# First layer of a two-block kernel: the state-space output is moved and used block by block from SyncE, and the first convolution taps go to ScalarE

## The reference, cut to what matters

```python
proj = x @ w_in                                   # 1024 -> 1536
xm, zm, us = proj[..., :512], proj[..., 512:1024], proj[..., 1024:]
xc = silu(causal_dwconv(xm, conv_w, conv_b))      # 4 taps
q, k, v = block-diagonal products of xc, xc, xm
gates = concat([q, k, v]) @ w_if + b_if
h = mlstm_chunkwise(q, k, v, i_pre, f_pre)
out_m = (layernorm(h) * mh_gain + skip * xc) * silu(zm)
y = gelu(s5_scan(us) + d_skip * us)
out_s = y * sigmoid(y @ w_glu + b_glu)
mix = concat([out_m, out_s]) @ w_out
```

## Time and profile before

| | |
|---|---|
| median of 3 runs | 2429.64 us (2429.21 to 2430.43) |
| the profiled execution | 2428.72 us, span 2426.9 us |
| mean granted TensorE clock | 0.995 |
| VectorE busy | 1456.6 us (60%) |
| ScalarE busy | 1077.9 us (44%) |
| GpSimd busy | 227.5 us (9%) |
| chain that ended last | PE 82%, DVE 12%, ACT 2%, waits for issue 1% |

### The profile page before, as it was taken

The page is one execution under the profiler, slowest core; times in us unless marked ns, Lnnn a source line. Parts: engine busy times, 40 slices in busy tenths (PEclk is TensorE's granted clock), DMA queues, the critical chain, the costliest instruction groups (busy, mean ns, idle before and its releaser), DMA issues.

```text
span 2426.9 us, 33037 instructions
## 1 busy us (share of the span) xinstructions
PE 2372.9 (98%) x11655; PEld 1940.0 (80%) x11655; DVE 1456.6 (60%) x2078; ACT 1077.9 (44%) x1456; POOL 227.5 (9%) x303
## 2 busy tenths in 40 slices
PE   8999999999999999999999999999999989999999
PEld 6766888888878878888888777888888867888887
DVE  7986654532677636545226856887533676787722
ACT  5346433332556645333225644554423573454421
POOL 2011100000100011000005231000011342000000
PEclk9999999999999999999999999999999999999999
DMA  7331233333222222333334202333333302333331
GB/s 176 70 96 52 79 104 92 96 95 98 71 84 71 78 70 82 100 95 91 96 99 120 57 10 87 104 104 95 91 100 117 103 10 70 87 104 95 91 96 65
DMA packets 403512, 212.31 MB, mean 87 GB/s; under 512 B 19411, under 2 KB 398935, under 8 KB 403431
## 3 DMA queue, kind: packets, MB, share of 16 engines
q1 hardware_dynamic: 397111, 199.65, 28.6%
q0 software_dynamic: 5984, 11.53, 2.0%
q10 hardware_dynamic: 336, 0.05, 0.0%
HBM read 204.38 MB, written 4.19 MB: 86 GB/s over the span
## 4 chain that ended last, share of the span: by engine, by line
PE 82%; DVE 12%; ACT 2%; issue 1%; DVEq 1%; DMA 0%; POOL 0%; ACTq 0%; SPq 0%
PE bank L708 68%; PE bank L754 4%; DVE tmp L1978 2%; PE bank L758 2%; DVE w_lo L1946 2%; PE bank L1336 1%; DVEq L1975 1%; PE bank L1310 1%; PE bank L784 1%; PE bank L1278 1%; DVE small L2731 1%; PE bank L1240 1%; PE bank L1149 0%; DVE tmp L1987 0%; PE bank L1203 0%
## 5 line engine op out<-in xcount | busy, mean ns | idle before, releaser
L1946 DVE TENSOR_TENSOR w_lo<-w_raw,w_hi 128x1024 fp32r<-128x1024 f32 x380 | 472.6, 1244 | 525.3 <-ACT w_hi L1410 520.5
L708 PE MATMUL bank<-h_hi,w_hi 128*128 128x512 f32 x1840 | 726.9, 395 | 1.9 <-DVE w_lo L1946 1.0
L708 PE MATMUL bank<-h_lo,w_hi 128*128 128x512 f32 x1840 | 718.4, 390 | 0.0
L708 PE MATMUL bank<-h_hi,w_lo 128*128 128x512 f32 x1840 | 718.0, 390 | 0.0
L1410 ACT ACTIVATE w_hi<-w_raw 128x1024 fp32r<-128x1024 f32 x380 | 401.9, 1059 | 630.5 <-PE bank L708 613.1
L708 PEld LDWEIGHTS bank<-h_hi,w_hi 128*128 128x128 f32 x1840 | 346.8, 188 | 77.7 <-issue 3.8
L708 PEld LDWEIGHTS bank<-h_lo,w_hi 128*128 128x128 f32 x1840 | 346.4, 188 | 72.6
L708 PEld LDWEIGHTS bank<-h_hi,w_lo 128*128 128x128 f32 x1840 | 346.8, 188 | 72.0 <-issue 1.9
L708 PE MATMUL bank<-hid_hi,w_hi 128*128 128x512 f32 x704 | 273.9, 389 | 0.0
L708 PE MATMUL bank<-hid_hi,w_lo 128*128 128x512 f32 x704 | 273.9, 389 | 0.0
L708 PE MATMUL bank<-hid_lo,w_hi 128*128 128x512 f32 x704 | 273.9, 389 | 0.0
(11 more groups left out here) (469 smaller groups left out, 2877.9 us busy)
## 6 DMA issues: line engine op xcount, KB each, us to landing
w_raw<-in_ffn_w SPq DMA_DIRECT2D x120, 512.0 KB, 3.8
w_raw<-in_w_up SPq DMA_DIRECT2D x88, 512.0 KB, 3.8
w_raw<-in_c_w_in SPq DMA_DIRECT2D x32, 512.0 KB, 4.0
w_raw<-in_w_down SPq DMA_DIRECT2D x32, 512.0 KB, 3.6
w_raw<-in_w_in SPq DMA_DIRECT2D x28, 512.0 KB, 3.9
w_raw<-in_w_o SPq DMA_DIRECT2D x16, 512.0 KB, 3.6
w_raw<-in_ab_w_in SPq DMA_DIRECT2D x12, 512.0 KB, 5.9
w_raw<-in_ffn_w SPq DMA_DIRECT2D x16, 384.0 KB, 3.2
```

The source lines that it names most:

```text
L708: mm = nc.tensor.matmul(out[:], w[:, s, k], v[:, kt], start=(kt == 0 and w is w_hi and v is hi), stop=(kt == sum(slabs) - 1 and v is lo))
L1946: nc.vector.tensor_tensor(w_lo[:, s], w_raw[:, s], w_hi[:, s].bitcast(F32), ALU.subtract).then_inc(lo_done, 1)
```

## The change

- The round trip of the S5 output is issued by SP, in four blocks. ScalarE sets `ys_ready` after each block. For each, SP loads the block of `us`, stores the block of `ys_step` with eight DMAs of a quarter of the former size, waits for them, and loads the block of `ys`. The code stands between the second and the third slab of `ab_w_out`. SP's loop over these slabs is written out, and POOL no longer takes part.
- ScalarE does the first tap (with the bias) of each tile of the convolution, one between every two blocks that it copies, then the four additions that make `lstm_bd[:, 3]`, and it clears `gate_w`. VectorE loses these instructions. The terms of the gate sum are computed in place in `lstm_wif`.
- VectorE's two weight splits in `turn_back` stand behind the convolution. `s5_gelu` on VectorE is cut in two, `skip_of_s5` and `low_of_s5`, and both stand ahead of `projections`. ScalarE's `s5_gelu` stands ahead of `lstm_gates`.
- TensorE waits a second time for `laid_out`, ahead of the value products. Two semaphores are joined in one, `first_turned`.

```diff
@@ SP, ab()
-                plain(a["ab_w_out"][0], 8)
+                w = cols(a["ab_w_out"][0])
+                for t in range(8):
+                    if t == 2:
+                        ys_blocks()
+                    load(w[:, :, t * P:(t + 1) * P])
+            def ys_blocks():
+                by_step = ys_dram.rearrange("(g p) j c -> j p g c", p=GW)
+                for i in range(4):
+                    tile, groups = slice(i * P, i * P + P), slice(8 * i, 8 * i + 8)
+                    sp.wait_ge(ys_ready, n(ys_ready))
+                    sp.dma_start(us[:, i], us_dram[tile]).then_inc(us_back, 16)
+                    for j in range(STEP):
+                        sp.dma_start(by_step[j][:, groups], ys_step[GW * j:GW * j + GW, groups]).then_inc(ys_stored, 16)
+                    sp.wait_ge(ys_stored, n(ys_stored, 16 * STEP))
+                    if i:
+                        sp.wait_ge(us_back, n.now(us_back))
+                        sp.wait_ge(ys_loaded, n.now(ys_loaded))
+                    n(us_back, 16)
+                    sp.dma_start(ys[:, i], ys_dram[tile].rearrange("p j c -> p (j c)")).then_inc(ys_loaded, 16)
+                    n(ys_loaded, 16)
@@ POOL
-            pool.wait_ge(ys_ready, 1)
-            for j in range(STEP):
-                pool.dma_start(by_step[j], ys_step[GW * j:GW * j + GW]).then_inc(ys_stored, 16)
-            pool.dma_start(us[:], us_dram.rearrange("(k p) i c -> p k i c", p=P)).then_inc(us_back, 16)
-            pool.wait_ge(ys_stored, 16 * STEP)
-            pool.dma_start(ys[:], ys_dram.rearrange("(k p) j c -> p k (j c)", p=P)).then_inc(ys_loaded, 16)
@@ TensorE, lstm_front()
+                pe.wait_ge(laid_out, n(laid_out))
                 for k in range(4):
                     out = take(5 + k % 3)
@@ ScalarE, s5_core()
+                act.wait_ge(s5["vector_to_pe"], n(s5["vector_to_pe"], 4))
+                nc.scalar.activation(gate_w[:].rearrange("p k g -> p (k g)").rearrange("p (k z) -> p k z", k=4),
+                                     lead[:, 0:P].unsqueeze(1).to_broadcast([P, 4, P]), ACT.Copy).then_inc(tap_ready, 1)
                 for i in range(4):
+                    act.wait_ge(s5["vector_to_pe"], n(s5["vector_to_pe"]))
+                    nc.scalar.activation(xc[:, i], xm[:, i], ACT.Identity, scale=col("conv_w", 12 + i), bias=col("conv_b", i))\
+                        .then_inc(tap_ready, 1)
+                    if i == 3:
+                        act.wait_ge(laid_out, n(laid_out))
+                        for k in range(4):
+                            nc.scalar.activation(lstm_bd[:, 3, k], lstm_bd[:, 2, k], ACT.Identity, bias=value_mean[:, k:k + 1])
+                        act.drain().then_inc(laid_out, 1)
                     act.wait_ge(s5["pe_to_scalar"], n(s5["pe_to_scalar"]))
                     nc.scalar.activation(ys_step[:, 8 * i:8 * i + 8], ...)
-                act.drain().then_inc(ys_ready, 1)
+                    act.drain().then_inc(ys_ready, 1)
@@ ScalarE, ab()
+                s5_gelu()
                 lstm_gates()
-                s5_gelu()
@@ VectorE, convolve()
                     for k in tiles:
-                        ts(xc[:, k], xm[:, k], col("conv_w", 12 + k), col("conv_b", k), ALU.mult, ALU.add)
-                    settle()
+                        dve.wait_ge(tap_ready, n(tap_ready))
@@ VectorE, s5_core()
                     turn_back(i)
-                    if i < 2:
-                        only_split(1)
@@ VectorE, lay_out()
-                step(nc.vector.memset(gate_w[:], 0.0))
-                for k in range(4):
-                    ts(lstm_bd[:, 3, k], lstm_bd[:, 2, k], value_mean[:, k:k + 1], None, ALU.add, None)
+                dve.wait_ge(tap_ready, n(tap_ready))
@@ VectorE, ab()
                 convolve()
+                skip_of_s5((0, 1))
+                only_split(2)
+                skip_of_s5((2, 3))
                 lower_exponents()
+                low_of_s5()
                 projections()
-                s5_gelu()
                 lstm_gates()
```

More of the change, by code:

```diff
@@ L276, in program @@
         gate_sum = small[:, 152:152 + 96].rearrange("p (m g) -> p m g", m=12)
-        gate_terms = tmp[:, 0, 0:12 * 32].rearrange("p (m e g) -> p m e g", m=12, e=4)
+        gate_terms = lstm_wif
         c_q = m("c_q", [P, SEQ], 16)
@@ L354, in program @@
             sem(k) for k in ("x_dev_ready", "x_hat_ready", "x_hat_turned", "x_raw_turned", "x_ready"))
-        s5_rows_turned = sem("s5_rows_turned")
-        gains_turned, par_turned, par_ready = sem("gains_turned"), sem("par_turned"), sem("par_ready")
+        first_turned, par_turned, par_ready = sem("first_turned"), sem("par_turned"), sem("par_ready")
+        tap_ready = sem("tap_ready")
         eps_ready = sem("eps_ready")
@@ L637, in _ @@
                 pool.dma_start(u_step[GW * k:GW * k + GW], by_step[i]).then_inc(us_loaded, 16)
-            pool.wait_ge(ys_ready, 1)
-            by_step = ys_dram.rearrange("(g p) j c -> j p g c", p=GW)
-            for j in range(STEP):
-                pool.dma_start(by_step[j], ys_step[GW * j:GW * j + GW]).then_inc(ys_stored, 16)
-            pool.dma_start(us[:], us_dram.rearrange("(k p) i c -> p k i c", p=P)).then_inc(us_back, 16)
-            pool.wait_ge(ys_stored, 16 * STEP)
-            pool.dma_start(ys[:], ys_dram.rearrange("(k p) j c -> p k (j c)", p=P)).then_inc(ys_loaded, 16)
             for norms in ((sq_mix,), (sq_in, sq_ffn), (sq_in, sq_mix), (sq_in, sq_ffn), (sq_in,)):
@@ L833, in _ @@
                     pe.wait_ge(gains_in, 16 * row_dmas[gains_in])
-                    nc.tensor.transpose(take(7)[:, 0:GAINS], rows[0:GAINS, 0], ident[0:GAINS, 0:GAINS]).then_inc(gains_turned, 1)
+                    nc.tensor.transpose(take(7)[:, 0:GAINS], rows[0:GAINS, 0], ident[0:GAINS, 0:GAINS]).then_inc(first_turned, 1)
                     for k in range(4):
@@ L875, in project @@
                 pe.wait_ge(s5_rows_in, 16 * 5)
-                nc.tensor.transpose(take(3)[:, 0:2 * GROUPS], s5_rows[:], ident[0:2 * GROUPS, 0:2 * GROUPS]).then_inc(s5_rows_turned, 1)
+                nc.tensor.transpose(take(3)[:, 0:2 * GROUPS], s5_rows[:], ident[0:2 * GROUPS, 0:2 * GROUPS]).then_inc(first_turned, 1)
                 product(h_hi, h_lo, [KD], 4)
@@ L2065, in s5_prepare @@
                 aim = par[:, ROWS["a_im"]:ROWS["a_im"] + GROUPS]
-                dve.wait_ge(s5_rows_turned, 1)
+                dve.wait_ge(first_turned, 2)
                 step(nc.vector.tensor_copy(par[:, ROWS["a_re"]:ROWS["a_re"] + 2 * GROUPS], bank[3][:, 0:2 * GROUPS]))
@@ L2277, in s5_core @@
                     turn_back(i)
-                    if i < 2:
-                        only_split(1)
             def lay_out():
                 dve.wait_ge(lstm_in, 16 * 9)
-                step(nc.vector.memset(gate_w[:], 0.0))
-                tt(gate_terms, lstm_w4[:].rearrange("p v k e -> p (v k) e").unsqueeze(3).to_broadcast([P, 12, 4, 8]), lstm_wif[:],
+                tt(gate_terms[:], lstm_w4[:].rearrange("p v k e -> p (v k) e").unsqueeze(3).to_broadcast([P, 12, 4, 8]), lstm_wif[:],
                    ALU.mult)
@@ L2293, in lay_out @@
                 settle()
-                step(nc.vector.tensor_reduce(gate_sum, gate_terms.rearrange("p m e g -> p m g e"), AX.X, ALU.add))
+                step(nc.vector.tensor_reduce(gate_sum, gate_terms[:].rearrange("p m e g -> p m g e"), AX.X, ALU.add))
                 settle()
@@ L2315, in projections, with skip_of_s5, low_of_s5 @@
                         flag(bank_free[b])
-            def s5_gelu():
-                dve.wait_ge(us_back, 16)
-                dve.wait_ge(ys_loaded, 16)
-                for k in range(4):
+            def skip_of_s5(tiles):
+                for k in tiles:
+                    dve.wait_ge(us_back, n(us_back, 16))
+                    dve.wait_ge(ys_loaded, n(ys_loaded, 16))
                     own(nc.vector.scalar_tensor_tensor(ys[:, k], us[:, k].rearrange("p i c -> p (i c)"), col("s5_d", k),
                                                        ys[:, k], ALU.mult, ALU.add), ys_in)
+            def low_of_s5():
                 for k in range(4):
@@ L2932, in _ @@
                 if t == 1:
-                    dve.wait_ge(gains_turned, 1)
+                    dve.wait_ge(first_turned, 1)
                     step(nc.vector.tensor_copy(par[:, 0:GAINS], bank[7][:, 0:GAINS]))
```

## The result

The changed kernel is slower. Its median is 2433.82 us (2432.60 to 2435.53, 12 runs) beside 2429.32 us for the kernel before on the same chip (12 runs): ratio 1.0023, 95% interval [1.0015, 1.0030]. The forecast was 2429.4 us; rival A had 2434.1. The profiled execution took 2435.05 us, with a span of 2433.3 us. That is 6.3 us above the profiled execution of before, where the medians are 4.5 apart; the twelve executions of each kernel spread over 2.9 and 3.9 us.

What follows compares the result with a forecast made beforehand. TensorE, busy 98% of the span, was taken to bound the kernel. Terms of -0.25, -0.9 and -0.5 us, plus 1.4 for the clock, gave -0.25 on 2429.64: 2429.4 us, range 2426.2 to 2433.9.

Steps and rivals of the forecast that it cites:

- rival A: SP's four blocks are a chain of dependent round trips, so slower: 2431.6 or, at the upper bound, 2434.1 us; chance 0.27.
- the round trip from SP: SP's load, eight stores, wait and load take 5.2 us a block; last `ys` load issued at 149.35, landing at 151.5.
- the upper bound: Landing of a 32 KB store at 3.3 us, the fastest of POOL's stores: block 6.3 us, last load landing at 156.4.
- The point at which it costs: SP's transfer costs from a block above 5.0 us and makes the whole change a loss at about 5.3.
- The clock: TensorE's new 4.4 us idle ahead of the scores brings about 3.4 us at half clock, priced at 1.4 us.
- First gain: Silus no longer wait for the convolution: TensorE's 1.45 us wait goes, gate matmuls end at 149.8, projections at 156.9.
- no new wait at `laid_out`: TensorE's second wait for `laid_out`, ahead of the value products at 142.39, costs nothing.
- blocks not late: ScalarE's taps and additions fit the gaps between its copies, the last ending at 137.7, ahead of the copy at 138.92.
- Behind it: VectorE enters `lstm_heads` about 4 us earlier relative to TensorE; waits of 0.9 us go and another 0.5 us comes.
- the terms: `glu` matmuls take 8.2 us in place of 9.0; `lstm_heads` waits of 0.9 go; bank 7 freed earlier gives 0.5.
- Rival C: Of 5 us more of waits on VectorE and ScalarE between 188 and 230 us, half goes: 2424.8 us; chance 0.08.
- Rival B: The clock stays and the transfers land in time: -2.3 us, 2427.3 us; chance 0.20.

Runs made afterwards that it cites:

- e2: Changed kernel without the 32 stores and the wait for them, `ys` loaded from the copy of `us`: median -2.36 us, ratio 0.9991 against the kernel before.
- e7: Kernel before with only the block-wise transfer from SP, every other order as before: median -0.42 us, ratio 0.9997 against the kernel before.
- e10: Changed kernel, same transfer, last skip term behind evacuations, gate rows, Exp and Ln ahead of fourth Gelu: median -4.86 us, ratio 0.9984 against the kernel before.
- e1: Changed kernel with VectorE's evacuations put back ahead of the last two skip terms and the low halves: median +1.86 us, ratio 1.0010 against the kernel before.
- e5: Changed kernel with unread matmuls in TensorE's waits ahead of the seventh projection (25) and the scores (16): median +4.50 us, ratio 1.0020 against the kernel before.
- e3: Changed kernel with 26 unread matmuls in TensorE's wait ahead of the seventh projection: median +6.32 us, ratio 1.0025 against the kernel before.
- e6: Changed kernel with e4's transfer, evacuations ahead of the last skip term, gate rows ahead of the last two Gelus: median -1.17 us, ratio 0.9993 against the kernel before.
- e8: Kernel before with only ScalarE's first taps and VectorE's changed work up to the convolution: median -0.83 us, ratio 0.9997 against the kernel before.
- e4: Changed kernel with SP issuing the next block's stores before waiting for this block's, POOL loading `us`: median +1.65 us, ratio 1.0005 against the kernel before.

## Why the prediction was wrong

*The step that failed* is the round trip from SP, "a block then occupies SP for 0.36 + 7 x 0.33 + 2.15 + 0.36 = 5.2 us". It was 5.96, 7.48 and 6.47. The last `ys` load was issued at 154.38, not 149.35: 5.0 us late. The larger error is in the issue: 0.48 us from store to store in place of 0.33, 1.0 us a block, 4 us over four. The prediction went down from a weight load by the number of pieces, and that fails: a store of 16 partitions in 128 pieces of 256 bytes takes 0.42 to 0.44 us to issue in the changed kernel, more than the whole 128-partition load did (0.37), while the `us` loads, 128 pieces too, take 0.34 to 0.43. The landing of the last store of a block (1.9 us in three of them, 3.3 in the second) adds 0.4 over the four, and the gaps around the loads 0.7. The landing of the stores lay in the range given, but its size was read too early as of no account: POOL's stores of 128 KB took 3.3 us at best, these of 32 KB 1.7, though on another queue. The last `ys` load was taken to land in 2.15 us too; these took 2.6 to 2.8, 0.6 us more, so VectorE had the last block at 157.2 in place of 151.5, and began its evacuations at 160.89 in place of 154.7. Rival A named the mechanism and the time, but put the price on the landing alone, where four of the five us are issue. Its 2434.1 for the upper bound is therefore in part luck; besides, that case lets the last load take 2.6 us where the others have 2.15, and with 2.15 its sum gives 2433.7. The point at which it costs, 5.0 us a block, was passed in every block.

The Trainium skill (DMA: Bandwidth & Descriptors, Rules for kernel authors) advises to coalesce, and that rule spoke against this change: 8 stores became 32. e2 bears it out where VectorE stands behind the transfer (a stage of -0.73 without the stores, +6.65 with them); in e7 and e10 the same 32 stores cost nothing. The fixed cost of about 2.0 us (same page, Anatomy of one DMA) led to an estimate of 5.1 us a block, below the 5.96 to 7.48 measured here. The page gives that figure for DMAs issued by GpSimd, and these are SyncE's.

*What stands behind the wait.* Two links were missed. The seventh projection needs bank 0, so TensorE stood from 155.2, not from 156.9; that brought the fall of the clock forward, but not the scores back. And the scores need bank 4, behind the fourth Gelu (e1). The prediction had the gate rows done at 160 "in time for VectorE" and didn't ask TensorE. In the changed kernel VectorE's chain is the later one; with it out of the way, e1 shows ScalarE's at 6.54 us.

*The clock.* The fall came as forecast. Taken at 1.4 us, it was about 1.8 (e5).

*First gain, no new wait at `laid_out`, blocks not late:* right. The projections began at 149.76 (149.8 forecast), and the fourth copy stood at 138.94.

*Behind it:* right. TensorE made up 2.1 us from the start of `glu` (+8.35) to the first numerators (196.23 against 190.01, +6.2); the terms were 0.8, 0.9 and 0.5. About 0.5 of it is lost again by the first load of the feed-forward weights (+6.68). The wait of the earlier trace rows is gone. Rival C fell: the waits of 1.2 and 0.9 us behind 188 us stayed as they were. Rival B's case, data in time, came out in e2 at -0.73 in the stage, with the clock falling all the same.

*What stays open:* why the second block's stores took 3.3 us to land; and how far a stage varies between executions of one kernel, since each was traced once. e1 shows that it matters: its median is 3.4 us below what its stage gives, where all others agree within 2.2, and its profiled execution (2434.07 us) was one of the two slowest of eleven, 3.9 above their median.

## What to carry to other kernels

Before a step is moved ahead on an in-order engine, list what stands behind it there and which buffers that work frees for others: here two banks, freed by two engines, hung on one late block. Moving the last block's skip term and Gelu, and all low halves, behind what TensorE needs sooner turned +4.5 us into -4.9 with the transfer unchanged. Price a DMA by its issue on its engine as well as by its landing, from a row of the same shape; cutting it in four here turned 8 issues of 0.62 us on POOL into 32 of 0.48 on SP. Time won by one engine is spent at the next wait unless the chain behind it is moved too (e3, e6, e8).

## What was not expected of the hardware

SyncE takes 0.48 us from one store of 16 partitions and 32 KB to the next (3.76 us for 8, 7.61 for 16), more than the 0.37 of a load of 512 KB. With more of them in flight it can be longer (5.22 and 4.20 us for the next two eights of e4). The length of a wait doesn't tell by itself whether the clock falls: one of 1.84 us in e4 left the next four projections at 1.98 us for four, full pace, while e6's 1.59 us, which closed a stretch of short products and small waits, was followed by 7 us at about half (0.55 and 0.50).
